# Two expert weights taken in ahead, and large turns before small ones, in a two-layer MoE inference kernel

## The reference, cut to what matters

```python
g_idx = argmax(u @ w_group + b_group)            # one of 4 groups
top_v, top_i = top_k(e_logits of that group, 2)  # two of its 4 experts
gates = one_hot(ids) * softmax(top_v) * p_group  # 16 experts, two used per token
hg = u @ w_gate[e]; hu = u @ w_up[e]             # 1024 x 512 each
h = silu(hg) * hu * gates
out = sum over e of h @ w_down[e]                # 512 x 1024
```

## Time and profile before

| | us |
|---|---|
| median of 3 runs | 1353.87 |
| lowest, highest | 1352.77, 1355.72 |
| profiled execution, its own time | 1366.17 |
| profiled execution, span from first to last instruction | 1364.3 |
| PE busy, share of the span | 1192.8, 87% |
| DMA bytes of the page, mean rate | 339.13 MB, 249 GB/s |

### The profile page before, as it was taken

How to read it: one execution, slowest core, us unless ns; L and a number is a source line. 1 busy time by engine, 2 the same in 40 slices (tenths; PEclk the granted TensorE clock), 3 DMA queues, 4 the chain that set the end, 5 groups by cost and what they waited for, 6 DMA issues and landing times.

```text
span 1364.3 us, 24736 instructions
## 1 busy us (share of the span) xinstructions
PE 1192.8 (87%) x10925; PEld 665.4 (49%) x10925; DVE 374.5 (27%) x927; ACT 219.4 (16%) x471; POOL 149.2 (11%) x162
## 2 busy tenths in 40 slices
PE   5399999968989989988888999998889999989854
PEld 2144333647565544544434665545556554445433
DVE  1201330375261110111155222666342111111115
ACT  2101401231131111111104111211021111111102
POOL 7001100021211000000010000223222000000010
PEclk9699999966989998998979999998999999989886
DMA  9977974800447999999936211010546999999931
GB/s 332 373 275 265 351 290 185 326 9 3 181 194 281 397 380 402 400 404 386 347 114 245 67 57 62 1 62 0 221 196 213 388 383 404 398 389 379 414 112 55
DMA packets 74436, 339.13 MB, mean 249 GB/s; under 512 B 6750, under 2 KB 17789, under 8 KB 59668
## 3 DMA queue, kind: packets, MB, share of 16 engines
q1 hardware_dynamic: 63032, 301.24, 57.5%
q0 software_dynamic: 10816, 35.90, 7.7%
q10 hardware_dynamic: 476, 0.34, 0.1%
HBM read 312.92 MB, written 24.53 MB: 247 GB/s over the span
## 4 chain that ended last, share of the span: by engine, by line
PE 70%; DMA 17%; DVE 6%; issue 3%; SPq 2%; POOL 1%; ACT 1%; POOLq 0%; DVEq 0%; ACTq 0%
PE ps L2064 18%; PE ps L1790 16%; PE ps L1710 15%; DMA ring<-in_moe_w_up 13%; PE ps L2086 6%; DMA ring<-in_ada_w 3%; PE ps L1733 3%; PE ps L2222 2%; PE ps L1703 1%; PE ps L2074 1%; SPq L599 1%; PE ps L2047 1%; PE ps L2193 1%; PE ps L1999 1%; PE ps L1751 1%
## 5 line engine op out<-in xcount | busy, mean ns | idle before, releaser
L2064 PE MATMUL ps<-ring,work 128*32 128x256 f32 x5248 | 338.9, 400 | 46.6 <-DMA ring<-in_moe_w_up 39.1
L2064 PEld LDWEIGHTS ps<-ring,work 128*32 128x32 f32 x5248 | 167.0, 114 | 162.2 <-issue 69.4
L1790 PE MATMUL ps<-uT,ring 128*128 128x384 f32 x640 | 216.3, 494 | 6.1 <-ACT uT L567 4.8
L1790 PEld LDWEIGHTS ps<-uT,ring 128*128 128x128 f32 x640 | 120.0, 192 | 94.5 <-issue 17.5
L2086 PE MATMUL ps<-ring,work 128*32 128x256 f32 x2624 | 156.6, 379 | 1.7 <-DVE work L1573 1.7
L2086 PEld LDWEIGHTS ps<-ring,work 128*32 128x32 f32 x2624 | 84.3, 110 | 58.8 <-DVE work L1573 2.1
L1573 DVE COPY work<-ps 128x128 f32<-128x128 f32 x82 | 23.9, 292 | 278.1 <-PE ps L2074 278.1
L1710 PE MATMUL ps<-ring,uT 128*128 128x512 f32 x192 | 87.1, 607 | 0.0
L1085 ACT ACTIVATE work<-ps 128x128 f32<-128x128 f32 x82 | 22.8, 278 | 385.0 <-PE ps L2064 385.0
L1569 DVE TENSOR_TENSOR work<-ps,work 128x128 f32<-128x128 f32 x82 | 23.9, 292 | 176.7 <-ACT work L1085 176.7
L1733 PE MATMUL ps<-ring,silc 128*32 128x512 f32 x384 | 49.4, 637 | 17.3 <-DMA ring<-in_ada_w 17.3
(11 more groups left out here) (299 smaller groups left out, 997.9 us busy)
## 6 DMA issues: line engine op xcount, KB each, us to landing
ring<-in_moe_w_down SPq DMA_DIRECT2D x32, 2048.0 KB, 16.6
ring<-in_moe_w_gate SPq DMA_DIRECT2D x32, 2048.0 KB, 14.4
ring<-in_moe_w_up SPq DMA_DIRECT2D x32, 2048.0 KB, 18.0
ring<-in_ada_w SPq DMA_DIRECT2D x24, 2048.0 KB, 9.8
ring<-in_rec_w_in SPq DMA_DIRECT2D x6, 2048.0 KB, 24.0
ring<-in_hy_w_in SPq DMA_DIRECT2D x6, 2048.0 KB, 10.8
y_rows<-work SPq DMA_DIRECT2D x72, 96.0 KB, 12.0
work<-x_rows POOLq DMA_DIRECT2D x16, 384.0 KB, 7.9
```

Of the source, the lines that this page charges most:

```text
L1790: ins = pe.matmul(bank(key)[0:rows, 0:T], w(k), uT[:, k, :], start=(k == 0), stop=(k == DC - 1))
L2064: ins = pe.matmul(bank(key)[32 * q:32 * q + 32, 0:2 * P].rearrange("p (a n) -> p a n", a=2), xg[:, u, k, 32 * i:32 * i + 32], ring[:, 3 * ...
```

## The change

Three things change. First, the turn order: `CAPS` becomes two fixed large turns, then seven large, then seven small; the rank arithmetic follows (four small DVE operations for three), and so do row offsets. Second, turn 2's gate and up weights go no longer to the ring but to memory that is idle in the stage: `uT`, which now lies behind `work`, and parts of `work`. They are issued in four pieces as soon as the ranks are known, the last of them in layer 0 after the scatter has read `utok`. Third, slots are assigned anew: turn 0 uses slots 2, 3, 4, turn 1 uses 0, 5, 1, turn 2 only slot 2 for its down weights; turn 3 uses 3, 4, 5 and turn 4 uses 0, 1, 2, and from there on it is as before. With turn 2's two slots saved, the loads of turns 3 and 4 are issued one event earlier each. The spare memory is used once in a layer. The branch for overflowing experts reloads `utok`; it is not entered with these inputs unless an expert overflows its rows, and its diff is left out here, as are the slots of the loads before the stage.

```diff
-CAPS = [CAP] * FIXED + [CAP, CAP2] * HALF
+CAPS = [CAP] * (FIXED + HALF) + [CAP2] * (RANKS - HALF)
...
-        uT = sb("uT", [P, DC, T])
...
-        work = sb("work", [P, WORK])
+        room = sb("work", [P, WORK + DC * T])
+        work = room[:, 0:WORK]
+        uT = room[:, WORK:].rearrange("p (k t) -> p k t", k=DC)
...
+        def moe_slot(p, kind):
+            if p < 2:
+                return ((2, 3, 4), (0, 5, 1))[p][kind]
+            return None if p == 2 and kind < 2 else 3 * (p % 2) + kind
...
+        def spare(l, kind, k):
+            if k >= 6:
+                return 3840 + 1024 * kind + 512 * (k - 6)
+            return ((2 * NT * D, 12288)[l], WORK)[kind] + 512 * k
...
+                def load_spare(kind, e, k0, k1):
+                    at = spare(l, kind, k0)
+                    sp.dma_start(room[:, at:at + 512 * (k1 - k0)].rearrange("p (k n) -> p k n", n=512),
+                                 moe_src(l, kind, e)[:, k0:k1, :]).then_inc(S("spare_loaded"), 16)
...
                 sp.wait_ge(S("turns_known"), l + 1)
-                for p in range(NE - 2):
-                    step(p)
+                e2 = turn_of(2)
+                load_spare(1, e2, 0, 6)
+                full(sp, ("xt", l, NT - 1, 1))
+                load_spare(1, e2, 6, 8)
+                load_spare(0, e2, 6, 8)
+                if l == 0:
+                    sp.wait_ge(S("x_rows_stored"), 16 * 2 * NT)
+                    full(sp, (l, 0, "X", 1))
+                load_spare(0, e2, 0, 6)
+                e3 = turn_of(3)
+                full(sp, (l, 0, "GU", TILES[0] - 1))
+                load_part(2, 2, e2)
+                load_part(3, 0, e3)
+                full(sp, (l, 0, "Y", TILES[0] - 1))
+                load_part(3, 1, e3)
+                store(0)
+                e4 = turn_of(4)
+                full(sp, (l, 1, "GU", TILES[1] - 1))
+                load_part(3, 2, e3)
+                load_part(4, 0, e4)
+                full(sp, (l, 1, "Y", TILES[1] - 1))
+                load_part(4, 1, e4)
+                store(1)
+                full(sp, (l, 2, "Y", TILES[2] - 1))
+                load_part(4, 2, e4)
+                store(2)
+                for p in range(3, NE - 2):
+                    (as step(p) before)
...
-                chain(v.tensor_scalar(base[:, FIXED:], rank, pair, float(BASES[FIXED]), ALU.mult, ALU.add))
-                chain(v.scalar_tensor_tensor(base[:, FIXED:], small[:, FIXED:], -(HALF * pair - CAP) / (CAP - CAP2), base[:, FIXED:],
+                v.tensor_scalar(base[:, FIXED:], rank, float(CAP), float(BASES[FIXED]), ALU.mult, ALU.add)
+                chain(v.tensor_scalar(late, rank, -float(HALF), 0.0, ALU.add, ALU.max))
+                chain(v.scalar_tensor_tensor(base[:, FIXED:], late, -float(CAP - CAP2), base[:, FIXED:], ALU.mult, ALU.add))
...
+                            if p == 2:
+                                one, two = (spare(l, kind, k) + q * P for kind in range(2))
+                                first = room[:, one:one + P]
+                                both = bass.AP(first.tensor, first.offset, [first.ap[0], (two - one, 2), first.ap[1]])
+                            else:
+                                both = ring[:, g:r + 1:r - g, at:at + P]
```

## The result

The changed kernel takes 1388.54 us (1387.16 to 1389.03, four runs) against 1354.2 us: 34.3 us more, a ratio of 1.0252, 95% interval 1.0234 to 1.027. I had forecast 1358.3 us and a range of 1347 to 1365. The sign was right, the size was not: the forecast loss was 4.4 us.

What follows compares the result with a forecast made beforehand. PE was taken to bound most of the program, transfers the start and the two expert stages. Landings and tails -7.5, turn 1's delays +5.9 and +6, gave +4.4 us on 1353.87: 1358.3 us, range 1347 to 1365.

Steps and rivals of the forecast that it cites:

- the delay d of turn 1: Turn 1 of each expert stage: its rows land late beside the spare load, 5.9 us (layer 0) and 6 (layer 1).
- upper bounds: Turn 1, scatter ending last of all beside the weights: delay 7.9 us in layer 0, up to 7.4 + 2.3 in layer 1.
- The tail in stage 0: Layer 0's turn 15, bound by the filter tap: 1.3 us less plus half of 2.4, 2.5 less (0 to 5).
- the landing: Turn 15's up weights land 1.3 us earlier in layer 0 and 1.8 in layer 1, before turn 1's delay.
- the sum of +4.4: Whole kernel: -7.5 us from landings and tails, plus 5.9 and 6 for turn 1's delay in the two layers.
- the tail and landing there: End of layer 1's stage: up weights land 1.8 us earlier, and turn 15 ends 1.9 earlier at equal landing.
- the lead is given back between turns 1 and 3: Both stages, at turn 3: of the 10.8 us lead, 1.3 us remain in layer 0 and 1.8 in layer 1.
- The lead is kept: Rival: both expert stages end 10.8 us earlier, 1332.3 us without turn 1's delay; chance 0.05.
- the slot count: Turns 3 to 5: spare memory serves once, so turn 5's gate load waits for turn 3 in both kernels.
- The rival with the alternating packets: Scatter and weights in turn 1 alternate by whole packets: delays 7.9 and 7.7 us, sum +8.1, 1362.0 us; chance 0.25.

Runs made afterwards that it cites:

- experiment 1: The kernel before, unchanged, profiled once more: 1356.32 us, ratio 1.0002, span 1354.3 us.
- experiment 2: The kernel before with large turns first only, old ring and no spare load: 1355.42 us, ratio 0.9996.
- experiment 10: The changed kernel with all four spare pieces issued once the scatter has landed, beside turn 1's row load: 1365.33 us, ratio 1.0073.
- experiment 3: The changed kernel with large and small turns alternating as before, so spare load and new slots alone: 1381.32 us, ratio 1.019.
- experiments 4 and 5: 4: changed kernel, spare pieces issued after turn 1's rows landed, 1355.07 us; 5: kernel before plus the spare pieces loaded, read by nobody, 1390.72 us.
- experiment 9: The changed kernel with the spare pieces cut by partitions into sixteen transfers, contiguous stretches still 12 or 4 KB: 1389.53 us, ratio 1.0248.
- experiment 6: The changed kernel with the spare pieces cut into sixteen transfers of 2 KB contiguous stretches: 1372.55 us, ratio 1.0132.

## Why the prediction was wrong

**The step that failed is the last term, "the delay d of turn 1".** I took d as 5.9 and 6, with upper bounds of 7.9 and 9.7. Turn 1's gate/up end, read from the first load that SP issues behind it, shows it as 12.9 and 19.6 us: in the changed kernel that is turn 3's down load at 456.66, 49.5 us after the scatter's start, and in experiment 1 turn 3's gate load, 36.6 us after it; in the second stage 56.1 against 36.5. Together 32.5 instead of 11.9, which is 20.6 too little. The parts:

| us | taken | measured, stage 0 and 1 |
|---|---|---|
| scatter ends later | 4 and 4 (at most 6 and 8.3) | 7.5 and 13.4 |
| row load, issue to PE | 7.9 | 9.1 and 10.2 |
| PE there after the scatter's start | 20.5 and 20.8 | 18.4 and 18.2 |
| turn 1 at the low clock | 2.3 | 2.6 and 2.1 |

The scatter is the largest. My upper bound had it end when all bytes beside it are through at the full rate. In stage 0 scatter and weights came at 312 and 368 GB/s from 410 to 415 and 415 to 420 us, and the scatter stood still for a while beside the first 12 KB packets. In stage 1 the bound itself was wrong: SP goes on issuing while the scatter is under way. Turn 2's down and turn 3's gate load went out at 1056.1 and 1056.7 us, 9 us before the scatter had landed, and 6.0 MB of weights passed before that, not 4.19. Between the ends of 0 and 6 I chose 4 by the row of row loads in a full stage, which is a row on small reads, not on a scatter. The third line is a fault of another kind: I took a slack from one execution that was 12 us above the median, and carried it over to the median as it was; 2.1 and 2.5 us of it were PE's gaps in turn 0 in that execution.

**The tail in stage 0, mis-sized.** Without d I forecast this stage 3.8 us shorter (1.3 by the landing, 2.5 by the tail); it is 5.5 us longer (18.4 - 12.9), and the order alone makes it 4.1 longer. The filter weights don't come earlier when PE does, and PE's idle time in a tile costs the clock as well. The 2.4 us at the low clock behind the tap, half of which I had counted as a gain, belonged to the first profile: in experiment 1 that tile took 1.93 us. In stage 1 the same sum gives -5.8 (13.8 - 19.6) against -3.7 forecast, so that the tail and landing there were right in sign and near in size. The three errors, 20.6 + 9.3 - 2.1 = 27.8 us, are what the sum of +4.4 lacks to the 32.1 that the stages became longer.

**What was right.** With large turns first the lead is given back between turns 1 and 3: the idle stretch is there, the stages of the changed kernel end as much later than in experiment 2 as turn 1 does (32.4 against 32.5 us in both together), and in experiment 10 only 1.0 and 1.5 us of some 4.7 are kept. "The lead is kept" had 0.05. What the slot count did not say is that this hangs on the new order: with alternating turns 4.0 and 5.2 us are kept in the profile of experiment 3. The order was thus not neutral beside the spare load; it cost the 9 us by which 34.3 exceeds 25.3. No run has the early load in alternating turns without the late rows, so what it could be worth is not measured. Large turns take 17.96 us (turn 3 to turn 4, 492.74 to 510.70) against 17.79, none waits from turn 2 to 9, and the small ones are bound by transfers; the waits begin at turn 10 in both stages, one earlier than forecast. (Before, the first of the six waits of each stage stood at turn 5, a small one, and not at a large turn as I had read.) Turn 3's end follows from turn 1's as forecast, 456.66 plus two large turns of 17.9 us, 492.5 against 492.74 measured. That a scatter beside weights was the place to fear was right as well, and experiments 4 and 5 make it more than an argument: remove it, and 33 us go; add only it, and 37 come. The rival with the alternating packets was nearest with 1362.0, and still 26.5 us short. It took 7.7 us for d in stage 1 where my own upper bound gave 9.7, and it counted the large pieces as if each were one packet; experiment 9 against 6 shows that the number of transfers does not matter. The rule named there, from the Trainium skill ("DMA: Bandwidth & Descriptors", Queues, rings and completion order), is round-robin between the queues, a whole packet at a time. The packet counts of experiment 6 agree with it except in the first microseconds; the Trainium skill speaks of packets of 9 to 17 descriptors typically, whereas here one packet of the trace was one contiguous stretch (0.27 MB in 150 packets, 1.8 KB each, some of 512 B and less among them), and so it was the stretches' length that set the shares.

**What stays open.** Why the scatter had no packet for some 2 us beside the first 12 KB piece, in both stages, and how much of the 34 us is that rather than the one-for-one sharing. Experiment 6 in stage 0 (18.5 us, hardly less than 19.7) says that packet length isn't all of it.

## What to carry to other kernels

Idle transfer time is only free for what nobody waits for behind it: before filling it with bulk loads, look for small transfers of another queue on whose landing an engine waits. Issued behind them the bulk did no harm here, but then nothing of the lead was left either, so count both before you start. A lead in a ring is worth what the ring can still hold: count at which event both versions have issued the same loads, and ask whether another edit moves that event: here large turns first made turn 3 end 6 us later. And take a slack from two executions, at least one of them at the median.

## What the runs showed of the hardware

- Once both were under way, two queues on the same engines shared them packet for packet (152 to 150, 114 to 112 and 58 to 56 in 2 us), with weights in packets of 2, 4 and 12 KB; cutting weights into 2 KB stretches gave a 4 KB scatter beside them 0.56 MB against 0.27 MB. When the weights began, the scatter had far fewer packets for 2 to 6 us: 0 to 49 beside 12 KB, 84 to 192 beside 2 KB.
- A scatter of 3.1 MB took until 18.1 us after its last issue beside 6.0 MB of weights, 4.7 us without.
- PE's first group of 32 behind the waits for rows took 3.57 to 3.64 us instead of 1.93, in both stages. Such a wait costs about 2 us more than itself.
